# Norm hand-overs of a two-block transformer kernel: squares and output gains on ScalarE, heads without condition items, no GpSimd in the norms

## The reference, cut to what matters

```
def first_block(x, ...):
    h = rms_norm(x, pre_mix_g);  z = h @ w_in
    ...                                   # attention over chunks, pooling
    x = x + rms_norm(m @ w_o, post_mix_g)
    h = rms_norm(x, pre_ffn_g)
    up = causal_dwconv(h @ w_up, conv_w, conv_b)
    y = (gelu(up[..., :D_FF]) * up[..., D_FF:]) @ w_down
    return x + rms_norm(y, post_ffn_g)

def second_block(x, c, ctx, ...):
    m = split(silu(c) @ w_ada + b_ada, 6)            # and the first two for ctx
    p_ctx = modulate(rms_norm(ctx, norm1_g), ...) @ w_in2[:, :KV_WIDTH]
    p = modulate(rms_norm(x, norm1_g), m[0], m[1]) @ w_in2
    ...                                   # two kinds of attention, merged
    x = x + m[2] * (merged @ w_out)
    h = modulate(rms_norm(x, norm2_g), m[3], m[4])
    return x + m[5] * ((silu(h @ w_fg) * (h @ w_fu)) @ w_fd)
```

## Time and profile before

| | |
|---|---|
| median of three runs | 3025.4 us (3024.79 to 3029.65) |
| profiled execution, its own time | 3029.62 us |
| its span | 3027.8 us |
| granted TensorE clock, mean | 0.983 |
| TensorE / VectorE / ScalarE / GpSimd busy | 95% / 64% / 52% / 26% |
| DMA, mean | 202 GB/s |

### The profile page before, as it was taken

One profiled execution on the slowest core, in us unless ns is written; L12 is line 12 of the kernel. 1 busy time (PEld: TensorE's weight loads), 2 busy tenths in 40 slices (PEclk: granted clock), 3 DMA queues, 4 the chain that ended last, 5 costly groups with the idle time before them and its releaser, 6 DMA issues.

```text
span 3027.8 us, 54772 instructions
## 1 busy us (share of the span) xinstructions
PE 2876.0 (95%) x19290; PEld 2625.7 (87%) x19290; DVE 1922.9 (64%) x2344; ACT 1563.5 (52%) x2279; POOL 797.0 (26%) x644
## 2 busy tenths in 40 slices
PE   7998799999999999899999999989989999999999
PEld 7998789998899988788888888789978888888888
DVE  5666778666678877533355666757786665555554
ACT  5555455445577653323344666665546654344443
POOL 3455433003344422112103422234434520000000
PEclk9999899999999999999999999999999999999999
DMA  7873756667777775344556654577767876666665
GB/s 261 270 255 123 238 174 215 187 182 232 242 247 244 246 235 184 98 145 145 157 159 186 199 165 153 179 230 238 238 216 239 267 236 184 191 187 186 183 188 166
DMA packets 175403, 610.63 MB, mean 202 GB/s; under 512 B 19200, under 2 KB 28800, under 8 KB 174912
## 3 DMA queue, kind: packets, MB, share of 16 engines
q1 hardware_dynamic: 161856, 589.37, 62.1%
...
q0 software_dynamic: 784, 2.88, 0.3%
...
## 4 chain that ended last, share of the span: by engine, by line
PE 71%; DVE 11%; ACT 7%; DMA 6%; issue 5%; DVEq 0%; ACTq 0%; SPq 0%; POOL 0%; POOLq 0%
PE acc L1579 20%; PE acc L1583 20%; PE acc L1581 10%; PE acc L1582 9%; DVE wlo L1021 4%; ACT whi L603 3%; DMA raw<-w_ada 2%; ACT cond_products L599 2%; PE acc L1567 1%; PE acc L1570 1%; PE acc L1569 1%; PE sums L1797 1%; PE acc L1577 1%; DVE conv_out L1116 1%; DMA raw<-w_fg 1%
## 5 line engine op out<-in xcount | busy, mean ns | idle before, releaser
L1021 DVE TENSOR_TENSOR wlo<-raw,whi 128x1024 fp32r<-128x1024 f32 x864 | 1141.1, 1331 | 884.1 <-ACT whi L603 881.9
L1583 PE MATMUL acc<-operand,wlo 128*128 128x256 f32 (+1 forms) x4848 | 1415.3, 292 | 0.0
L603 ACT ACTIVATE whi<-raw 128x1024 fp32r<-128x1024 f32 x864 | 908.8, 1057 | 978.0 <-PE acc L1583 578.0
L1581 PE MATMUL acc<-operand,whi 128*128 128x256 f32 (+1 forms) x3168 | 953.0, 301 | 79.3 <-DVE wlo L1021 46.3
L1583 PEld LDWEIGHTS acc<-operand,wlo 128*128 128x128 f32 x4848 | 934.8, 193 | 15.6
L1582 PE MATMUL acc<-operand,whi 128*128 128x256 f32 (+1 forms) x3168 | 942.7, 298 | 0.0
L1581 PEld LDWEIGHTS acc<-operand,whi 128*128 128x128 f32 x3168 | 615.3, 194 | 104.0 <-issue 47.0
L1582 PEld LDWEIGHTS acc<-operand,whi 128*128 128x128 f32 x3168 | 615.8, 194 | 13.6
L1579 PE MATMUL acc<-operand,whi 128*128 128x512 f32 x1680 | 602.1, 401 | 14.0 <-DVE operand L1354 7.7
L457 POOL TENSOR_TENSOR cond_products<-cond_products 128x512 f32<-128x512 f32 x192 | 254.3, 1325 | 1257.0 <-ACT cond_products L599 1255.6
L1579 PE MATMUL acc<-ffn_act,whi 128*128 128x512 f32 x1344 | 473.4, 396 | 4.2 <-DVE wlo L1021 4.1
...
## 6 DMA issues: line engine op xcount, KB each, us to landing
raw<-w_ada SPq DMA_DIRECT2D x256, 512.0 KB, 4.4
...
```

Source lines behind the costliest of these rows:

```text
L603: act.activation(whi[j % RING][:], raw[j % RING][:], ACT.Copy).then_inc(hi_done, 2 if st.entries[j % st.upb - 1] == (None, ADA_VEC) else 1)
L1021: dve.tensor_tensor(wlo[j % RING][:], raw[j % RING][:], whi[j % RING][:].bitcast(F32), ALU.subtract).then_inc(lo_done, 2 if prev[0] is Non ...
L1581: pe.matmul(out_, h[:, x, f], mov[:, 0], start=first, stop=False)
L1583: ins = pe.matmul(out_, l[:, x, f], mov[:, 0], start=False, stop=last)
```

## The change

- The heads of w_in, w_up, the GLU, and a new head of the key stage (`kv_head`, two groups across) carry no condition item; up1a grows from 3 to 5 bodies with an item, a stage `up1c` of one body with an item is split off, up1b shrinks from 8 to 5 bodies without, the GLU gets one more body with and one less without, the keys have 5 instead of 6.
- In w_o, down2 and out ScalarE squares each group (`post`), from PSUM in w_o, and in the first two also multiplies it by the output gain; VectorE only adds the squares. The last group's squares are not added up: TensorE sums `RS` and the two squares in three matmuls. In the last body ScalarE does that work before it writes the high half of the fourth unit of the next head.
- Norm products are VectorE's alone; x = x + y is one operation per block. The blocks are 2, 2, 4, 4 and 4 tiles (`BLOCKS`), the last one inside the head's body, behind its second position (`then`); TensorE waits for operand tiles by twos. In the modulated norms ScalarE makes the high half from the product directly, with gain and offset, beside VectorE's shifts.
- The sum of squares inside a head still follows its sixth unit (place 5 now, place 8 before); the squares of the first norm are made inside the head's body, one chunk per place.
- In the key head TensorE runs two context units, the sum of squares, two more context units, the same four units for x, and then four units for both at once ("both").
- The tables and the context are loaded from GpSimd's queue, behind ScalarE's first high half of w_in's and up1a's first unit; GpSimd's memset follows the items of w_in.

The diff, cut (eight columns of indentation left out):

```diff
-    st_inh = Stage("w_in_head", cols("w_in", 0, 0, GW), 2, 4, "scale", ada=1, op=0, across=True)
+    st_inh = Stage("w_in_head", cols("w_in", 0, 0, GW), 2, 4, "scale", op=0, across=True)
...
-    st_up1h = Stage("up1_head", pairs("w_up", "w_up", 0, DFF), 2, 4, "conv", ada=1, op=32, across=True)
-    st_up1a = Stage("up1a", pairs("w_up", "w_up", GW, DFF + GW), 6, 4, "conv", ada=1, tile0=2, feat0=2)
-    st_up1b = Stage("up1b", pairs("w_up", "w_up", 4 * GW, DFF + 4 * GW), 2 * n1 - 8, 4, "conv", tile0=8, feat0=8)
+    st_up1h = Stage("up1_head", pairs("w_up", "w_up", 0, DFF), 2, 4, "conv", op=32, across=True)
+    st_up1a = Stage("up1a", pairs("w_up", "w_up", GW, DFF + GW), 10, 4, "conv", ada=1, tile0=2, feat0=2)
+    st_up1c = Stage("up1c", pairs("w_up", "w_up", 6 * GW, DFF + 6 * GW), 2, 4, "conv", ada=1, tile0=12, feat0=12)
+    st_up1b = Stage("up1b", pairs("w_up", "w_up", 7 * GW, DFF + 7 * GW), 2 * n1 - 14, 4, "conv", tile0=14, feat0=14)
...
-    st_kv = Stage("kv", cols("w_in2", 0, 0, GW), KVW // GW, 4, "kv", ada=1, op=64)
+    st_kvh = Stage("kv_head", cols("w_in2", 0, 0, GW), 2, 4, "kv", op=64, across=True)
+    st_kv = Stage("kv", cols("w_in2", 0, 2 * GW, GW), KVW // GW - 2, 4, "kv", ada=1, tile0=8)
...
-    st_u1a = Stage("glu1a", pairs("fg", "fu", GW, GW), 14, 4, "glu", ada=1, tile0=2)
-    st_u1b = Stage("glu1b", pairs("fg", "fu", 8 * GW, 8 * GW), 2 * n1 - 16, 4, "glu", tile0=16)
+    st_u1h = Stage("glu1_head", pairs("fg", "fu", 0, 0), 2, 4, "glu", op=120, across=True)
+    st_u1a = Stage("glu1a", pairs("fg", "fu", GW, GW), 16, 4, "glu", ada=1, tile0=2)
+    st_u1b = Stage("glu1b", pairs("fg", "fu", 9 * GW, 9 * GW), 2 * n1 - 18, 4, "glu", tile0=18)
...
-ACC = {1: 1, 3: 2, 4: 3, 6: 4}
+BLOCKS = ((0, 2), (2, 2), (4, 4), (8, 4), (12, 4))
...
 def _(pool):
-    pool.wait_ge(in_att, 64)
-    pool.memset(XC32[64:128, 0:4, :, 1, 192:256], -1e30).then_inc(masked, 1)
-    pool.wait_ge(masked, 1)
+    pool.wait_ge(hi_done, unit(st_in, 0, 0) + 1)
+    for kt in range(4):
+        pool.dma_start(XC32[:, kt, :, 1, :], bass.AP(
+            rel.tensor, 2 * kt * rel.shape[1], [[1, P], [rel.shape[1], 2], [1, S]])).then_inc(in_att, 16)
+    pool.dma_start(XC32[:, 13, :, 1, :], cst[:, C_FLIP:C_FLIP + 512].rearrange(
+        "p (a n) -> p a n", a=2)).then_inc(in_cst, 16)
+    pool.dma_start(R[:, 32:40, :], pool_w).then_inc(in_cst, 16)
...
-    add_condition(st_inh)
     add_condition(st_in)
+    pool.wait_ge(ada_ops, st_o.ib * ADA_OPS + 1)
+    pool.wait_ge(in_att, 64)
+    pool.memset(XC32[64:128, 0:4, :, 1, 192:256], -1e30).then_inc(masked, 1)
+    pool.wait_ge(masked, 1)
...
     for c in range(2):
         pool.dma_start(XC32[:, 8 * c:8 * c + 8, 0, 1, :], ctxT[:, 8 * c:8 * c + 8, :]).then_inc(in_ctx, 16)
-    pool.wait_ge(ada_ops, st_up1h.ib * ADA_OPS + 1)
-    normed_chunks(1, 0)
-    add_condition(st_up1h)
     add_condition(st_up1a)
+    add_condition(st_up1c)
     pool.wait_ge(sq_ready, SQ[5][0])
...
+        elif st.kind in SUMMED:
+            tile = b * (2 * st.GB) + 2 * gb
+            gain = {"mix_out": "post_mix", "down2": "post_ffn"}.get(st.kind)
+            act.wait_ge(evac_done, g + 2)
+            if st.kind == "mix_out":
+                act.wait_ge(used, grouped(st, b, gb))
+                source = PS[:, gb % 2, :, 0:S]
+            else:
+                act.wait_ge(vstep, vst(st, b, gb, 1))
+                source = (X if st.kind == "out" else R)[:, ds(tile if st.kind == "out" else tile + Yt, 2), :]
+            act.activation(Cb[:], source, ACT.Square).then_inc(astep, 1)
+            if gain is not None:
+                if st.kind == "down2":
+                    act.wait_ge(astep, ast(st, b, gb, 0))
+                for m in range(2):
+                    y = R[:, ds(tile + Yt + m, 1), :].rearrange("p a n -> p (a n)")
+                    ins = act.activation(y, PS[:, gb % 2, m, 0:S] if st.kind == "mix_out" else y, ACT.Copy,
+                                         scale=V[:, ds(tile + VEC[gain] + m, 1)])
+                ins.then_inc(astep, 1)
     def low_half(st, b, gb):
...
+            closing = final and st.kind in SUMMED and j - RING == st.last[-1]
+            if closing:
+                post(st, b, st.GB - 1)
             if j < st.upb or not final:
                 hi(st, b, j, before, b + st.ib)
...
-            if norm is not None and at == 8:
+            if at in then:
+                then[at]()
+            if norm is not None and at == 5:
                 root(norm)
...
-    for c in range(4):
-        square_chunk(c, 0)
-    for kt in range(4):
-        act.dma_start(XC32[:, kt, :, 1, :], bass.AP(
-            rel.tensor, 2 * kt * rel.shape[1], [[1, P], [rel.shape[1], 2], [1, S]])).then_inc(in_att, 16)
-    act.dma_start(XC32[:, 13, :, 1, :], cst[:, C_FLIP:C_FLIP + 512].rearrange(
-        "p (a n) -> p a n", a=2)).then_inc(in_cst, 16)
-    act.dma_start(R[:, 32:40, :], pool_w).then_inc(in_cst, 16)
     act.wait_ge(cleared, 1)
-    body(st_inh, 0, norm=0)
+    body(st_inh, 0, final=True, norm=0, then={c: lambda c=c: square_chunk(c, 0) for c in range(4)})
...
+    def modulated_hi(m, base, blocks):
+        for i in blocks:
+            k0, n = BLOCKS[i]
+            act.wait_ge(mod_t, modulated(m, i))
+            for kt in range(k0, k0 + n):
+                ins = act.activation(XC[:, kt, 0, 0, :], R[:, Yt + kt, :], ACT.Identity, scale=GS[:, kt:kt + 1],
+                                     bias=MOD[:, base + kt:base + kt + 1])
+            ins.then_inc(mod_hi, 1)
...
+    def up_chunk(c):
+        for kt in range(4 * c, 4 * c + 4):
+            act.wait_ge(x_new, kt + 1)
+            act.activation(XC[:, kt, 0, 0, :], X[:, kt, :], ACT.Copy,
+                           scale=V[:, VEC["pre_ffn"] + kt:VEC["pre_ffn"] + kt + 1]).then_inc(op_hi, 1)
+        square_chunk(c, Yt)
+    for c in range(3):
+        up_chunk(c)
+    body(st_up1h, 0, final=True, norm=2, then={1: lambda: up_chunk(3)})
     run(st_up1a)
     act.wait_ge(in_ctx, 32)
     act.activation(XC32[:, :, 1, 1, :], XC32[:, :, 0, 1, :], ACT.Square).then_inc(sq_ready, 1)
+    body(st_up1c, 0, final=True)
     run(st_up1b)
...
-    modulated_hi(1, 0)
+    modulated_hi(1, 2 * ADA_CTX, range(4))
+    body(st_kvh, 0, final=True, then={1: lambda: modulated_hi(1, 2 * ADA_CTX, (4,))})
     run(st_kv)
...
+        if k in SUMMED:
+            squared, final = ast(st, b, gb, 0), ast(st, b, gb, A_STEPS[k] - 1)
+            did, settled = steps_from(st, b, gb, V_STEPS[k] - 1)
+            if closing:
+                dve.wait_ge(astep, final)
+                dve.sem_inc(vstep, 1)
+                dve.sem_inc(evac_done, 1)
+                return
+            dve.wait_ge(astep, squared)
             did(dve.tensor_tensor(RS[:], RS[:], Cb[:, 0, :], ALU.add))
             settled()
+            dve.wait_ge(astep, final)
             dve.tensor_tensor(RS[:], RS[:], Cb[:, 1, :], ALU.add).then_inc(evac_done, 1)
...
+    def add_normed(k0, n, i):
+        y = R[:, Yt + k0:Yt + k0 + n, :]
+        dve.tensor_tensor(y, y, rep(RS[:], n), ALU.mult).then_inc(y_normed, n)
+        dve.wait_ge(y_normed, KT * i + k0 + n)
+        dve.tensor_tensor(X[:, k0:k0 + n, :], X[:, k0:k0 + n, :], y, ALU.add).then_inc(x_new, n)
...
-    clear(Zp[:, :, 0:2])
-    for c in range(4):
-        add_normed(c, 0, "post_mix")
-        for kt in range(4 * c, 4 * c + 4):
-            scaled_lo(kt, gain_col("pre_ffn", kt), 2 * KT + kt + 1, X[:, kt, :])
-    body(st_up1h, 0, norm=2)
+    for k0, n in BLOCKS[:4]:
+        up_chunk(k0, n)
+    body(st_up1h, 0, final=True, norm=2, then={1: lambda: up_chunk(*BLOCKS[4])})
...
+    def scale_block(m, i):
+        k0, n = BLOCKS[i]
+        dve.tensor_tensor(R[:, Yt + k0:Yt + k0 + n, :], X[:, k0:k0 + n, :], rep(RS[:], n),
+                          ALU.mult).then_inc(mod_t, 1)
...
+        dve.wait_ge(mod_t, modulated(m, i))
+        for kt in range(k0, k0 + n):
+            last = dve.tensor_scalar(XC32[:, kt, 1, 0, :], R[:, Yt + kt, :], GS[:, kt:kt + 1],
+                                     MOD[:, base + kt:base + kt + 1], ALU.mult, ALU.add)
+        last.then_inc(mod_v, 1)
...
+    def modulate(m, base, blocks):
+        for i in blocks:
+            scale_block(m, i)
+            if i - 1 in blocks:
+                low_block(m, i - 1)
+            shift_block(m, i, base)
+        low_block(m, blocks[-1])
...
-        add_normed(c, 1, "post_ffn")
+        add_normed(4 * c, 4, 1)
     invert(5)
-    dve.wait_ge(mods_done, st_kv.ib + 1)
-    modulate(1, X, 0, "norm1", 2 * ADA_CTX, 3)
+    modulate(1, 2 * ADA_CTX, range(4))
+    body(st_kvh, 0, final=True, then={1: lambda: modulate(1, 2 * ADA_CTX, (4,))})
...
+            if own and st is not st_ba and x % 2 == 0:
+                pe.wait_ge(opnd, st.op + kt + 2)
...
         if i in ACC:
-            pe.wait_ge(acc_ready, ACC[i])
-            ins = pe.matmul(NB[:, 0:S], ones, XC32[:, 0, 1, 1, :] if i == 3 else RS[:], start=True, stop=True)
+            st = ACC[i]
```

(17 more changed lines are left out.)

170 lines of the change are left out of this document (62 added, 108 removed).

## The result

The changed kernel takes **2989.5 us** (median of 4 runs, 2988.4 to 2991.0) where the kernel before takes 3027.5 us (4 runs, 3024.8 to 3032.7): the ratio is 0.9877, with a 95% interval of 0.9864 to 0.9890. Predicted were 2991 us. The profiled execution has a span of 2986.8 us against 3027.8, and a granted clock of 0.991 against 0.983.

The account below looks back on a forecast made before the run. TensorE, busy 95% of the span, was taken to bound the kernel, with 87 us left over around the norms to work on. Gains of 50.4 us less costs (a) to (f) gave -34.5 us, 2991 us, range 2979 to 3012 us.

Parts of the forecast that it names:

- The heads: Start, norm after w_o, keys and GLU: shorter stretches won 8.3, 17.9, 15.7 and 8.5 us, 50.4 us together.
- the forecast's signs: Changed profile: head stretches of about 32, 42, 61 and 34 us, first operand matmul 8 to 9 us after w_o.
- The stop of over 5 us: Sign of a wrong forecast: a stall over 5 us in the first body behind a head, from the moved transfers.
- (a): Condition items moved out of four heads: three more conv bodies and one GLU body carry one, +9.1 us.
- (b): ScalarE's added squares and scaled copies in w_o, down2 and out: -0.5 to +5 us, taken as +2.
- the slower rival: ScalarE bounds w_o, down2 and out: 1.9 us for each of 24 groups, 45 us, total 3034 us; chance 0.03.
- (c): Tables and context sent from GpSimd's queue behind the next stage's first unit: 0 to 6.6 us each, 2 taken for both.
- (d): First group's matmuls in w_o and out wait every two tiles, not four: 0 to 2 us, taken as 0.5.
- (f): Semaphore delays of four hand-made schedules: 0 to 8 us, taken as 2.0.
- (e): Context's squares now before a conv body with a condition item: 0 to 2 us, taken as 0.3.
- The third rival: More than forecast: added condition bodies free, (b) to (f) nil, -46.4 us, total 2979 us; chance 0.10.

Follow-up runs that it names:

- experiment 8: Kernel before with GpSimd's position-table wait and memset behind w_in's condition items, not ahead of the first: 3019.7 us (1 run).
- experiment 7: Changed kernel with the six table transfers issued on ScalarE's queue ahead of the first body, not on GpSimd's: 2986.0 us (1 run).
- experiment 3: Changed kernel with the last group of the three projections ahead of a norm summed by VectorE's two adds again: 2997.0 us (1 run).
- experiment 2: Kernel before with only the norm products that GpSimd multiplied given to VectorE: 3010.5 us (1 run).
- experiment 9: Changed kernel with the context's two transfers issued at w_o's second group again, not behind the head of the up projection: 2989.4 us (1 run).
- experiment 1: Changed kernel with ScalarE's square of the context issued one body later, behind up1c: 2977.0 us (4 runs), ratio 0.9850 to the kernel before.
- experiment 12: Changed kernel with context's square one body later, root and reciprocal ahead of the fourth split, ten constant matmuls in the GLU's wait: 2978.6 us, ratio 0.9844.

## Why the prediction was right

The time (2991 for 2989.5 us) is right, and its sum too, but one of its terms is far off and others, set too high, make up for it. That they do so almost to the microsecond is luck. So is part of the 1.5 us: the forecast took 34.4 us off a median of 3025.4, the median of four runs is 3027.5, and the gain by the medians is 38.1 us (33 to 41 by the interval of the ratio).

**The heads.** Predicted were 8.3, 17.9, 15.7 and 8.5 us, 50.4 in all; measured 7.8, 17.6, 17.3 and 8.9 us, 51.6. The keys give 1.6 us more. After w_o the first operand matmul was set 8.6 us behind w_o's end, and it is 8.7. The start was put down to the condition buffer that GpSimd holds (experiment 8 shows it: 3.7 us) and in part to the transfers, and these are worth nothing (experiment 7). What the chain alone gives (experiment 3: 5 to 6 us), GpSimd's absence (experiment 2: 8.3 us), the keys' order (9.4 us) and the finer blocks (3.5 us) were each tried singly. What the norm after w_o owes to the context's move is 2.0 us (experiment 9). The head stretches are 32.6, 42.7, 59.3 and 33.9 us, where the forecast's signs had 32, 42, 61 and 34. The stop of over 5 us that was to be a sign of being wrong came too, not in the first body behind a head but in the sixth.

**(a) Condition items moved, +9.1.** From the head's end to the first item of down1 the up projection takes 317.9 us in place of 302.9, with three bodies more that carry an item. Of these 15.0 us, 9.7 are what experiment 1 removes, and 5.3 are left. But the kernel before has its own stop of 2.41 us there, where experiment 1's kernel has 0.23, so the three items cost 5.3 + 2.2 = 7.5 us, for 8.1 predicted. In this 1.3 us come back in the first body behind the head, 25.9 us in place of 27.2. Behind the GLU's head it is 734.4 in place of 732.8 us, +1.6 for an expected 1.05; this stretch differs by 2 us and more between executions, so that part is not shown. Together 9.1, so the term holds as far as it can be read.

**(b) ScalarE in the output stages, +2.** Three bodies of w_o take 73.0 in place of 71.6 us, down2 115.0 in place of 115.9, `out` 73.0 in place of 72.9. So +0.6, no more than chance (w_o takes 72.4 and 72.6 in the two variants of the kernel before), and the slower rival, which needed 1.5 us for each of 24 groups, is far away. The upper bound was also added up wrong: half of 8 x 1.58 us is 6.3 us, not 5. The Trainium skill's word on ScalarE and simple arithmetic (Trainium Architecture — The Big Picture, "The five engines, in one table") names VectorE as up to about 3 times as fast per element; for this shape no such difference is seen: ScalarE's square has 0.60 us for 128x512, VectorE's product 0.69.

**(c) Moved transfers, +2.** Nothing is seen of the context's behind the head, and the tables' (experiment 7) 0. **(d)** was not tried alone. **(f)** no stretch has 2 us left for it.

**(e) The context's squares ahead of a body with an item, +0.3: this step failed.** It says "The context's squares now come before a conv body with a condition item: 0 to 2 us". The body takes 36.0 us against 26.4 with the squares behind it (experiment 1), 9.7 us; against the kernel before, which lost 2.2 us of this already, the move cost 7.5 us. I had counted ScalarE's 3.6 us only. The square releases GpSimd's adds, the adds hold VectorE for 9.5 us, and VectorE's splits feed TensorE. That GpSimd's work holds VectorE was in the earlier trace rows, 3.40 for 1.21 us, and I used it for the norms; I did not ask where else GpSimd adds. The kernel before showed it, 4.47 us for an operation of 0.17 us (L1303), and the prediction does not use it.

**The rest.** 9.1 + 2 + 2 + 0.5 + 0.3 + 2 = 15.9 us of costs were predicted, and 9.1 + 0.6 + 7.5 = 17.2 are found. So the stretches give -51.6 + 17.2 = -34.4 us, and predicted were -34.5. The profiled executions differ by 41.0 us. Most of the other 6.6 us lies where the code is the same: from the end of the keys to the end of `out` the profiled kernel before takes 760.6 us and the changed one 755.4, but the two variants of the kernel before of experiments 2 and 8 take 753.2 and 755.0, and the kernel of experiment 12 takes 759.2. So these 5 us are how one execution differs from another and no part of the change. The third rival's price, -46.4 us, takes 4 us of costs that no term of it gives; its size is about that of experiment 1's kernel, whose ratio of 0.9850 is 45 us.
